# A hybrid decoder layer on one NeuronCore: SSD chunks and attention woven into the input projections, the first routing put behind chunk 0, two output projections cut into pieces

## The chip, the core and the metric

The kernel runs on one NeuronCore of one Trainium2 chip, as one launch. The metric is the device time of that launch in microseconds (us): the median of three runs.

## What is computed

One decoder layer in float32, for 512 tokens of width 1024:

```python
h = x + concat(attention, ssd) @ w_out            # of rms_norm(x) @ w_in
h = h + peer(rms_norm(h))
out = rms_norm(h)

# attention: 8 query heads, 2 key/value heads of 64, a causal window of 128, bias and sinks
# ssd: causal depthwise conv of 4 taps and silu, then a Mamba-2 scan of 8 heads in 4 chunks of 128
#      tokens: inside a chunk (CB * decay) @ X, between chunks a state; gated by silu(z), rms_norm
def peer(xn, ...):
    q = (xn @ w_query).reshape(b, s, 8, 2, 128)
    s1, s2 = q[..., 0, :] @ sub_keys1.T, q[..., 1, :] @ sub_keys2.T
    v1, i1 = top_k(s1, 16); v2, i2 = top_k(s2, 16)
    top_s, pos = top_k(v1[..., :, None] + v2[..., None, :], 16)   # of the 256 sums
    idx = i1 * 128 + i2 at pos
    # per token and head 16 experts: gelu(expert_down[idx] . xn) * softmax(top_s) * expert_up[idx]
```

For every token 8 x 16 = 128 experts are fetched. An expert is one row of 2048 floats (down and up side by side, 8 KB).

## The kernel before

The 512 tokens are four tiles of 128, one token to a partition. The work has two parts.

**Prologue.** TensorE turns x (L754) and multiplies it with w_in in blocks of 128 columns that stream through five ring buffers: 8 blocks for the convolution, a narrow one for dt (L780), 5 for keys and queries, 4 for z and 1 for v (L788, L792). Then a loop over the four chunks c (TensorE from L865, VectorE from L609, ScalarE from L350) does, in the order in which each engine's program is written, the SSD scan and the attention of the chunk, and beside them the output projection of the chunk before it (`out_half`, L811, 16 matmuls of 512 columns, L817). In chunk 2 (`ROUTED`) tile 0 is normalized, turned, and its first query is made (`query`, L829; `keyed`, L839); in chunk 3 VectorE searches the sums and writes the first indices (`search_sums`, `search_indices`). w_out (4 MB) and w_query (8 MB, one transfer into `wq`) are loaded at L224 and L225, when all projections are done.

**Expert phase.** A tile has 128 slots, the launch 512 (`NS`). For slot s GpSimd issues an indirect DMA that gathers one expert for each of the 128 tokens, 1 MB, into one of ten row buffers (L272); VectorE takes 128 dot products (`group`, L686), ScalarE their gelu (L396), VectorE the gate (L692), ScalarE a diagonal matrix (L401), and TensorE adds diagonal x up into two PSUM banks (`expert`, L955, two matmuls of 512 columns). The two matmuls release the row buffer (`row_free`). A group is 4 slots (`GROUP`). 16 slots share one query q of 32; between the groups stand the query, the keys and the search of q+2 or q+3, in pieces. Every instruction order is written out by hand; an engine runs its program in order and stops at each wait.

GpSimd has nothing but constants and the gathers, in the order of s. Before slots 0 to 6 it also waits until the buffer's earlier contents are dead; the last of these waits is for all four output projections:

```python
                elif s == 6:
                    gp.wait_ge(sem("wo_ps"), NT)
                if s >= RING_E:
                    gp.wait_ge(sem("row_free"), s - RING_E + 1)
```

## Time and profile before

| | |
|---|---|
| median of 3 runs | 1587.43 us (1584.71 to 1587.95) |
| profiled execution, its own time | 1586.41 us |
| its span in the profile | 1584.7 us |
| TensorE busy, matmul | 1378.7 us (87%) |
| VectorE / ScalarE / GpSimd busy | 1063.1 (67%) / 390.4 (25%) / 620.3 us (39%) |
| gathers | 512, 536.90 MB, 82.0% of the span of the 16 DMA engines |
| mean granted TensorE clock | 0.945 of full |

The span is the time from the first to the last instruction of the profiled execution; its own time has 1.7 us more around it. A float32 matmul shows as two records. Ends of matmuls are modelled, so a busy TensorE is not one at its peak. L numbers are lines of the kernel before.

### The profile page before, as it was taken

The page shows a single profiled execution, that of the slowest core. Times are in us where ns is not written, and L with a number is a line of the kernel's source. Part 1 is how long each engine was busy: PE and PEld are TensorE (multiplying, and loading weights), DVE is VectorE, ACT ScalarE, POOL GpSimd, SP SyncE. Part 2 cuts the span into 40 slices and gives each one's busy share as a digit, 9 for nine tenths or more (in the row PEclk, how much of TensorE's full clock was granted, in tenths as well). Part 3 has the DMA queues.
Part 4 walks back from the last instruction along what each step waited for, and adds up shares of the span by engine and source line. Part 5 has one row for each costly group of instructions (what it writes and reads, how often), then busy time and mean ns, then how long its engine had stood idle before and what let it go on. Part 6 is the DMA issues. An engine that isn't in the chain of part 4 may idle for free.

```text
span 1584.7 us, 13883 instructions
## 1 busy us (share of the span) xinstructions
PE 1378.7 (87%) x4480; PEld 721.8 (46%) x4480; DVE 1063.1 (67%) x2655; ACT 390.4 (25%) x1041; POOL 620.3 (39%) x528
## 2 busy tenths in 40 slices
PE   8899999998888888888889888888888878888787
PEld 4359776554444444444444443434444434444233
DVE  4322667687676677777767677677677777667654
ACT  2013443222222222222222221222222222222122
POOL 0000001354444454455544454444454445444541
PEclk9999999999999999899999998999999999999988
DMA  5410702999999999999999999999999999999996
GB/s 166 126 56 25 297 36 91 367 408 421 421 422 421 421 422 421 410 421 421 401 422 421 415 422 413 421 421 412 421 415 420 418 403 417 421 412 420 421 405 260
DMA packets 84380, 568.71 MB, mean 359 GB/s; under 512 B 10035, under 2 KB 12372, under 8 KB 17748
## 3 DMA queue, kind: packets, MB, share of 16 engines
q0 software_dynamic: 73728, 536.90, 82.0%
q1 hardware_dynamic: 10580, 30.93, 5.8%
q8 instruction: 35, 0.57, 0.1%
q14 instruction: 37, 0.30, 0.0%
HBM read 564.13 MB, written 3.67 MB: 358 GB/s over the span
## 4 chain that ended last, share of the span: by engine, by line
DMA 45%; PE 35%; DVE 12%; ACT 3%; issue 2%; POOL 2%; SPq 0%; DVEq 0%; ACTq 0%
DMA arena<-in_experts_du_dram,arena 42%; PE ps L955 21%; DVE arena L686 6%; PE ps L788 4%; PE ps L817 3%; POOL arena L272 2%; PE ps L792 2%; PE ps L835 2%; DMA line_scratch<-arena 2%; ACT arena L401 1%; DVE arena L692 1%; ACT arena L396 1%; ACT arena L282 1%; PE ps L937 1%; PE ps L780 1%
## 5 line engine op out<-in xcount | busy, mean ns | idle before, releaser
L955 PE MATMUL ps<-arena 128*128 128x512 f32 x2048 | 980.1, 635 | 180.3 <-ACT arena L401 179.6
L272 POOL DMA_INDIRECT arena<-in_experts_du_dram,arena x512 | 618.3, 1208 | 938.8 <-PE ps L955 604.9
L686 DVE CUSTOM_DVE_ANT_0 arena<-arena 128x1024 f32<-128x1024 f32 x512 | 618.4, 1224 | 320.2 <-DMA arena<-in_experts_du_dram,arena 314.5
L955 PEld LDWEIGHTS ps<-arena 128*128 128x128 f32 x2048 | 406.3, 203 | 711.2 <-issue 475.5
L396 ACT ACTIVATE arena<-arena 128x4 f32<-128x4 f32 (+2 forms) x131 | 26.9, 205 | 913.6 <-DVE arena L686 913.6
L401 ACT ACTIVATE arena<-ident,arena 128x128 f32<-128x128 f32 x512 | 163.9, 390 | 40.5 <-DVE arena L692 39.0
L835 PEld LDWEIGHTS ps<-arena,wq 128*128 128x128 f32 x1024 | 119.2, 192 | 15.1 <-issue 14.3
L835 PE MATMUL ps<-arena,wq 128*128 128x128 f32 x1024 | 119.6, 275 | 0.5 <-ACT arena L282 0.5
L788 PE MATMUL ps<-arena 128*128 128x512 f32 x208 | 94.7, 617 | 7.0 <-DMA arena<-in_w_in_blocks_dram 5.4
L788 PEld LDWEIGHTS ps<-arena 128*128 128x128 f32 x208 | 41.0, 199 | 59.4 <-issue 57.4
L282 ACT ACTIVATE arena<-ps 128x256 f32<-128x256 f32 (+1 forms) x114 | 51.7, 453 | 54.3 <-PE ps L835 27.9
L817 PE MATMUL ps<-arena 128*128 128x512 f32 x128 | 55.9, 594 | 1.4 <-ACT arena L282 1.4
L692 DVE SCALAR_TENSOR_TENSOR arena<-arena 128x4 f32<-128x4 f32 (+2 forms) x131 | 29.1, 222 | 38.3 <-ACT arena L396 38.3
L497 DVE TENSOR_TENSOR arena<-ps,arena 128x512 f32<-128x512 f32 x13 | 9.0, 692 | 63.7 <-PE ps L788 57.9
L686 DVE DVE_READ_ACCUMULATOR2_ANT arena<- 128x1 f32 x512 | 41.9, 82 | 0.0
L396 ACT ACT_TABLE_LOAD x32 | 41.1, 1283 | 0.6
L390 ACT ACT_TABLE_LOAD x31 | 39.8, 1283 | 0.6
L817 PEld LDWEIGHTS ps<-arena 128*128 128x128 f32 x128 | 24.0, 190 | 30.3 <-issue 28.7
L792 PE MATMUL ps<-arena 128*128 128x128 f32 x320 | 36.3, 275 | 0.0
L792 PEld LDWEIGHTS ps<-arena 128*128 128x128 f32 x320 | 36.1, 192 | 0.5 <-issue 0.5
L844 PEld LDWEIGHTS ps<-arena 128*128 128x128 f32 x128 | 19.2, 191 | 15.2 <-issue 14.8
L602 DVE TENSOR_TENSOR arena<-arena 128x512 f32<-128x512 f32 x32 | 22.5, 702 | 1.1
(153 smaller groups left out, 702.1 us busy)
## 6 DMA issues: line engine op xcount, KB each, us to landing
arena<-in_w_in_blocks_dram SPq DMA_DIRECT2D x18, 512.0 KB, 7.1
wq<-in_w_query_dram SPq DMA_DIRECT2D x1, 8192.0 KB, 33.5
arena<-in_experts_du_dram,arena POOLq DMA_INDIRECT x512
arena<-in_w_out_dram SPq DMA_DIRECT2D x1, 4096.0 KB, 14.0
h<-in_x_dram SPq DMA_DIRECT2D x4, 512.0 KB, 5.3
out_dram<-arena SPq DMA_DIRECT2D x8, 256.0 KB, 7.6
line_scratch<-arena SPq DMA_DIRECT2D x1, 1536.0 KB
arena<-line_scratch SPq DMA_DIRECT2D x1, 1024.0 KB, 5.7
```

Of the source, the lines that this page charges most:

```text
L272: gp.indirect_dma_start(rows[s % RING_E], None, experts_du, bass.IndirectOffsetOnAxis(ap=idx[:, (q // PH) % 2, q % PH * TOPK + i:q % PH * ...
L282: link(act, nc.scalar.activation(o, i, func, **kw), name, n)
L390: nc.scalar.activation(eg[:, q % 2], tdiff[:, q % 2], ACT.Exp, accum_out=gsum[:, q % 2, 0:1]).then_inc(sem("gate_exp"), 1)
L396: nc.scalar.activation(gel[:, part], pre[:, part], ACT.Gelu).then_inc(sem("gelu"), 1)
L401: nc.scalar.activation(diag[:, s % 8, :], ident[:], ACT.Copy, scale=actv[:, s % 16:s % 16 + 1]).then_inc(sem("diag"), 1)
L686: v.tensor_tensor_reduce(down, down, xn2[q // PH % 2], 1.0, 0.0, ALU.mult, ALU.add, pre[:, s % 16:s % 16 + 1]).then_inc(sem("dots"), 1)
L692: v.scalar_tensor_tensor(actv[:, part], gel[:, part], gsum[:, q % 2, 1:2], eg[:, q % 2, part], ALU.mult, ALU.mult).then_inc(sem("act_ready ...
L788: last = mm(bank[:], w[:, k, :], xnT[:, k, :], start=(k == 0), stop=(k == KT - 1))
L792: last = mm(bank[:, t * P:(t + 1) * P], xnT[:, k, t * P:(t + 1) * P], w[:, k, :], start=(k == 0), stop=(k == KT - 1))
L817: last = mm(ps[WO_BANKS[c][b]][:], mixT[c][:, k, :], wo[:, k, b * 512:(b + 1) * 512], start=(k == 0), stop=(k == KT - 1))
L835: last = mm(ps[2 + q % 2][:, j * P:(j + 1) * P], wq[:, k, col:col + P], xn2T[:, k, :], start=(k == 0), stop=(k == KT - 1))
L955: last = mm(ps[4 + 2 * (t % 2) + b][:], diag[:, s % 8, :], up[:, b * 512:(b + 1) * 512], start=False, stop=False, skip_group_check=True)
```

## The change

- **Projections.** v and dt become one step of 136 columns (`project_values`), right behind the convolution's blocks. The first block is multiplied tile by tile between the turns of x. The write of the bias line to DRAM and its reading back are two places of SyncE's order instead of one.
- **Chunks.** The loop over chunks is gone; its parts are functions that are called in a written order, and chunk 0 and the start of chunk 1 stand between the projections of k, q and z. On GpSimd four element-wise operations per chunk take work from VectorE: `skip`, `state_decay`, `add_off`, `gate`.
- **Routing.** Output projection 0 is in the middle of chunk 1; tile 0 is normalized, queried and searched during chunk 2. Slots 0 and 1 are worked off before the attention of chunk 3.
- **Output projections 2 and 3** are 32 single matmul pieces, one behind each pair of slots of the first four queries. VectorE adds a finished half to h behind the eighth pair. Output projection 1 stays whole.
- **Loads.** w_query is in eight blocks of 1 MB. 0 and 1 are loaded in the projections, 2 and 3 before the first gather, 4 and 5 when slots 1 and 2 are free, 6 and 7 and the two norm weights of 512 KB behind the last output projection.
- **Buffers.** Twelve row buffers: slots 0 to 9 use ten of them once, slots 10 to 65 go round eight (`EARLY_RING`), slots from 66 (`JOIN`) round ten (`FULL_RING`). Buffers 10 and 11 lie where w_out was; slot 66 waits for the last output projection.
- **Groups** have 2 slots in the first four queries, then 4 as before. In the expert phase query and keys are made for q+2 (before: q+3), and the first two thirds of the search stand in one piece behind the last group.

```diff
+HALF_RING = 8
+JOIN = 66
+N_BUF = 12
+def buffer_of(s):
+    if s < 10:
+        return s
+    if s < JOIN:
+        return EARLY_RING[(s - 10) % HALF_RING]
+    return FULL_RING[(s - JOIN) % 10]
+EARLY_RING = [0, 3, 4, 5, 6, 7, 8, 9]
+FULL_RING = [10, 11, 0, 3, 4, 5, 6, 7, 8, 9]
+    _sizes = [2] * 8 if _q < 4 else [4] * 4 if _q < NQ - 1 else [4, 4, 2, 2, 2, 1, 1]
...
 SyncE
+            for q in (4, 5):
+                sp.wait_ge(sem("row_free"), q - 2)
+                sp.dma_start(w_head[q], w_query[q].rearrange("p (k c) -> p k c", k=KT)).then_inc(sem(f"wq_in{q}"), 16)
+            sp.wait_ge(sem("wo_half"), 2 * NT)
+            for q in (6, 7):
+                sp.dma_start(w_head[q], w_query[q].rearrange("p (k c) -> p k c", k=KT)).then_inc(sem(f"wq_in{q}"), 16)
+            sp.dma_start(w_ffn, norm_ffn.to_broadcast([P, D])).then_inc(sem("wffn_in"), 16)
             sp.dma_start(w_fin, norm_final.to_broadcast([P, D])).then_inc(sem("wffn_in"), 16)
...
 GpSimd
+            def gate(c):
+                gp.wait_ge(sem("diag_read"), c + 1)
+                gp.wait_ge(sem("zv_out"), NT * NT)
+                link(gp, g.tensor_tensor(yb[:, c, :], yb[:, c, :], zs[c], ALU.mult), "gated", n)
...
-                elif s == 6:
-                    gp.wait_ge(sem("wo_ps"), NT)
-                if s >= RING_E:
-                    gp.wait_ge(sem("row_free"), s - RING_E + 1)
+                elif s == 3:
+                    gp.wait_ge(sem("mixS_ready"), NT)
...
+                elif s == 6:
+                    gp.wait_ge(sem("pv_ps"), NT)
+                elif s == 8:
+                    gp.wait_ge(sem("mixS_ps"), NT)
+                elif s == JOIN:
+                    gp.wait_ge(sem("wo_half"), 2 * NT)
+                if LAST_USER[s] is not None:
+                    gp.wait_ge(sem("row_free"), LAST_USER[s] + 1)
...
 VectorE, the expert phase
+            def add_projection(c, b):
+                dve.wait_ge(sem("wo_half"), 2 * c + b + 1)
+                half = slice(512 * b, 512 * b + 512)
+                go(v.tensor_tensor(h[:, c, half], h[:, c, half], ps[WO_BANKS[c][b]][:], ALU.add), "h_mixed")
...
             for q in range(NQ):
                 t, r = divmod(q, PH)
+                for i, (s0, n_slots) in enumerate(GROUPS[q]):
+                    if s0:
+                        group(q, s0, n_slots)
+                    done = s0 + n_slots - q * TOPK
+                    if t == 0 and r < 4 and i % 8 == 7:
+                        add_projection(2 + r // 2, r % 2)
+                    if done == 4 and q and q + 1 < NQ:
+                        search_indices(q + 1)
...
+                    if done == 16:
+                        if q + 2 < NQ:
+                            search_halves(q + 2)
+                            search_sums(q + 2)
...
 TensorE, the end of the prologue and the expert phase
+            turn_mix(2)
+            ssd_diagonal(3)
+            out_half(1, 0)
+            add_residual(0)
+            experts(*GROUPS[0][0])
+            turn_probs(3)
+            attend(3)
+            out_half(1, 1)
+            turn_mix(3)
             for q in range(NQ):
                 t, r = divmod(q, PH)
+                for i, (s0, n_slots) in enumerate(GROUPS[q]):
+                    if s0:
+                        experts(s0, n_slots)
+                    if t == 0 and r < 4:
+                        out_piece(2 + r // 2, r % 2, i)
+                    done = s0 + n_slots - q * TOPK
+                    if done == 4 and q + 2 < NQ:
+                        query(q + 2)
+                    if done == 8 and q + 2 < NQ:
+                        keyed(q + 2)
```

**GpSimd, from the constants to the gathers.** Rows give a line, an operation, tiles written and read, size and the semaphores waited for. Before:

```order
L251 MEMSET arena 128x3 [waits const] x8
L272 DMA arena<-in_experts_du_dram,arena 128x2048 [waits nat_ps,routed,const]
L272 DMA arena<-in_experts_du_dram,arena 128x2048 [waits score_sb]
L272 DMA arena<-in_experts_du_dram,arena 128x2048 [waits y_ps]
L272 DMA arena<-in_experts_du_dram,arena 128x2048 [waits pv_ps]
L272 DMA arena<-in_experts_du_dram,arena 128x2048 [waits mixT_ps]
L272 DMA arena<-in_experts_du_dram,arena 128x2048
L272 DMA arena<-in_experts_du_dram,arena 128x2048 [waits wo_ps]
```

Now, from `skip(3)` to the gather of slot 8 (`wide` and `arena` hold the row buffers):

```order
L317 TENSOR_TENSOR wide<-arena,hrow 128x512 [waits nat_sb,gated]
L359 DMA wide<-in_experts_du_dram,arena 128x2048 [waits step_ps,routed,y_skip]
L359 DMA arena<-in_experts_du_dram,arena 128x2048 x2
L324 TENSOR_TENSOR state<-state,sm 128x512 [waits state_ready,decays,off_ps]
L330 TENSOR_TENSOR wide<-wide,arena 128x512 [waits off_read,state_dec]
L336 TENSOR_TENSOR wide<-wide,arena 128x512 [waits zv_out,diag_read,y_off]
L359 DMA wide<-in_experts_du_dram,arena 128x2048 [waits mixS_ready,gated]
L359 DMA arena<-in_experts_du_dram,arena 128x2048 [waits score_sb]
L359 DMA arena<-in_experts_du_dram,arena 128x2048 [waits y_ps]
L359 DMA arena<-in_experts_du_dram,arena 128x2048 [waits pv_ps]
L359 DMA arena<-in_experts_du_dram,arena 128x2048
L359 DMA arena<-in_experts_du_dram,arena 128x2048 [waits mixS_ps]
```

Three gathers stand ahead of the last chunk's operations, the others behind them, and the chunk's norm (`mixS_ready`) is waited for by slot 3.

**VectorE, between the last slots of a query and the first of the next, in the first four queries.** Each `ISA arena<-arena 128x1024` is the dot product of one slot. Before (the last group of query 0, the halves of a search, the next group):

```order
L686 ISA arena<-arena 128x1024 [waits row5]
L686 ISA arena 128x1
L692 SCALAR_TENSOR_TENSOR arena<-arena 128x4 [waits gelu]
L569 MAX arena<-arena 128x8 [waits s_sb]
...
L584 CAST arena<-arena 128x32 [waits half1,half0]
L686 ISA arena<-arena 128x1024 [waits row6,dve_step]
```

Now (the last pair of query 1, the finished half, the search, the next pair):

```order
L852 SCALAR_TENSOR_TENSOR arena<-arena 128x2 [waits gelu]
L775 TENSOR_TENSOR h<-h,ps 128x512 [waits wo_half]
L800 MAX arena<-arena 128x8 [waits s_sb,h_mixed]
...
L818 TENSOR_TENSOR arena<-arena 128x256 [waits dve_step]
...
L826 TENSOR_SCALAR arena<-arena 128x16 [waits dve_step]
L846 ISA arena<-arena 128x1024 [waits row8]
L846 ISA arena 128x1
L846 ISA arena<-arena 128x1024 [waits row9]
L846 ISA arena 128x1
L850 RECIPROCAL arena<-arena 128x1 [waits gate_exp]
L852 SCALAR_TENSOR_TENSOR arena<-arena 128x2 [waits gelu,dve_step]
```

The add that waits for `wo_half` stands ahead of the search and of the next query's first pair.

**TensorE at the same place** (L1193 the experts, four rows to a pair; L1142 a piece of an output projection). Before there is no output projection in this stretch (L955 the experts). Now:

```order
L1193 MATMUL ps<-arena 128x512 x4
L1142 MATMUL ps<-wide,arena 128x512
L1193 MATMUL ps<-wide,arena 128x512 x4
L1142 MATMUL ps<-wide,arena 128x512
L1193 MATMUL ps<-arena 128x512 x4
L1142 MATMUL ps<-wide,arena 128x512
L1171 MATMUL ps<-arena 128x128 x16
```

The eighth piece of a half, which raises `wo_half`, comes behind the eighth pair of its query, and the next pair follows at once.

## Rows read from the trace of the kernel before

**Rows 1.** The page: GB/s in 40 slices of 39.6 us, and the chain's shares.

```profile
GB/s 166 126 56 25 297 36 91 367 408 421 421 422 421 421 422 421 410 421 421 401 422 421 415 422 413 421 421 412 421 415 420 418 403 417 421 412 420 421 405 260
...
DMA 45%; PE 35%; DVE 12%; ACT 3%; issue 2%; POOL 2%; SPq 0%; DVEq 0%; ACTq 0%
```

**Rows 2.** Busy time by window: engines' us and counts, clock granted, DMA share, GB/s.

```profile
0.00:294.00 294.00, 275.51 (x1317) 183.08 (x1318) 143.55 (x341) 81.01 (x190) 12.33 (x26) 0.98 0.37 124
...
314.00:318.00 4.00, 4.00 (x6) 1.87 (x7) 3.93 (x7) 1.07 (x4) 0.24 (x1) 0.62 1.02 426
```

**Rows 3.** Timeline of GpSimd: start, us, what, idle before and releaser.

```profile
1.09 0.29 POOL L245 TENSOR_SCALAR_AFFINE_SELECT ident<-ones 128x128 f32<-128x128 f32 x1
...
265.82 1.53 POOL L272 DMA_INDIRECT arena<-in_experts_du_dram,arena  x1 [262.60 <-DVE arena L606]
...
288.68 0.94 POOL L272 DMA_INDIRECT arena<-in_experts_du_dram,arena  x1 [13.02 <-PE ps L817]
...
1559.45 0.94 POOL L272 DMA_INDIRECT arena<-in_experts_du_dram,arena  x1 [0.78 <-PE ps L955]
```

**Rows 4.** Timeline of VectorE: dot products of slots 6, 66, 510 and 511.

```profile
294.19 1.22 DVE L686 CUSTOM_DVE_ANT_0 arena<-arena 128x1024 f32<-128x1024 f32 x1 [4.25 <-DMA arena<-in_experts_du_dram,arena]
...
447.28 1.23 DVE L686 CUSTOM_DVE_ANT_0 arena<-arena 128x1024 f32<-128x1024 f32 x1 [1.25 <-DMA arena<-in_experts_du_dram,arena]
...
1570.62 1.23 DVE L686 CUSTOM_DVE_ANT_0 arena<-arena 128x1024 f32<-128x1024 f32 x1 [0.72 <-DMA arena<-in_experts_du_dram,arena]
...
1573.08 1.22 DVE L686 CUSTOM_DVE_ANT_0 arena<-arena 128x1024 f32<-128x1024 f32 x1 [0.74 <-DMA arena<-in_experts_du_dram,arena]
```

**Rows 5.** Timeline of TensorE (two records to a matmul).

```profile
4.41 1.94 PE L754 MATMUL ps<-ident,h 128*128 128x128 f32 x8 [4.41 <-DMA h<-in_x_dram]
7.50 5.38 PE L754 MATMUL ps<-ident,h 128*128 128x128 f32 x24 [1.15 <-DMA h<-in_x_dram]
...
79.30 8.49 PE L780 MATMUL ps<-arena 128*128 128x8 f32 x64
...
251.75 13.95 PE L817 MATMUL ps<-arena 128*128 128x512 f32 x32
...
288.24 3.73 PE L835 MATMUL ps<-arena,wq 128*128 128x128 f32 x32
...
293.53 0.61 PE L844 MATMUL ps<-arena 128*128 128x128 f32 x4
293.98 13.90 PE L955 MATMUL ps<-arena 128*128 128x512 f32 x32
...
443.77 15.48 PE L955 MATMUL ps<-arena 128*128 128x512 f32 x32 [4.54 <-ACT arena L401]
```

**Rows 6.** Timeline of VectorE: chunk work (segments, norm from first to last, scores, maxima).

```profile
192.33 0.69 DVE L668 CUSTOM_DVE_ANT_0 arena<-arena 128x512 f32<-128x512 f32 x1
...
195.16 0.75 DVE L670 SCALAR_TENSOR_TENSOR arena<-arena,sm,wn 128x512 f32<-128x512 f32 x1
...
208.73 2.15 DVE L627 TENSOR_SCALAR arena<-ps,sm 128x128 f32<-128x128 f32 x8
...
215.33 2.87 DVE L650 SCALAR_TENSOR_TENSOR arena<-ps,arena 128x512 f32<-128x512 f32 x4
218.23 2.29 DVE L652 TENSOR_REDUCE sm<-arena 128x8 f32<-128x2048 f32 x1
```

**Rows 7.** Timeline of VectorE: a search from first to last, an add, a dot's end.

```profile
299.32 0.48 DVE L569 MAX8 arena<-arena 128x8 f32<-128x128 f32 x2
...
305.22 0.43 DVE L595 TENSOR_SCALAR arena<-arena 128x16 f32<-128x16 f32 x1
...
308.12 0.17 DVE L606 SCALAR_TENSOR_TENSOR arena<-arena 128x16 int32<-128x16 f32 x1
...
313.41 0.68 DVE L547 TENSOR_TENSOR h<-h,ps 128x512 f32<-128x512 f32 x1
...
441.50 1.22 DVE L686 CUSTOM_DVE_ANT_0 arena<-arena 128x1024 f32<-128x1024 f32 x1
```

More of the change, by code:

```diff
@@ L39 @@
 SLOTS = PH * TOPK
-GROUP = 4
-RING_E = 10
 NS = 4 * SLOTS
@@ new lines, in _ @@
+            values()
+            dt_exps()
+            ssd_start(0)
+            ssd_decay(0)
+            softmax(0)
+            gates_z(0)
+            gates_z(1)
+            turned(0)
+            ssd_start(1)
+            gates_z(2)
+            gates_z(3)
+            ssd_decay(1)
+            mixed(0)
+            softmax(1)
+            squared(0)
+            turned(1)
+            ssd_start(2)
+            transposed(0)
+            ssd_decay(2)
+            query(0)
+            softmax(2)
@@ new lines, in scores @@
+            def scores(c, part):
+                k0 = 0 if c else P
+                if c and part == 0:
+                    dve.wait_ge(sem("pv_ps"), c)
+                if c == 0 and part == 0:
+                    dve.wait_ge(sem("bias_in"), 16)
+                dve.wait_ge(sem("score_ps"), 2 * c + part + 1)
+                for i in range(2):
+                    b = 2 * part + i
+                    src = ps[B_ATT[i]][:].rearrange("p (h k) -> p h k", h=2)
+                    go(v.scalar_tensor_tensor(prob[:, 2 * b:2 * b + 2, k0:], src[:, :, k0:], float(HD) ** -0.5,
+                                              bias[:, 2 * b:2 * b + 2, k0:], ALU.mult, ALU.add), "score_sb")
@@ L749, in _, with turn_x @@
             pe.wait_ge(sem("const"), LOADS["const"])
-            for t in range(NT):
+            def turn_x(t):
                 pe.wait_ge(sem(f"x_in{t}"), 16)
@@ new lines, in _ @@
+            mm(ps[4][0:HEADS, 0:LW], rb[:], buckets, start=True, stop=True).then_inc(sem("line_ps"), 1)
+            for n_step in range(1, NXB):
+                project(n_step)
+            project_values()
+            project(S_K)
+            ssd_start(0)
+            project(S_Q)
+            ssd_segments(0)
+            ssd_state(0)
+            project(S_Q + 1)
+            ssd_diagonal(0)
+            project(S_Q + 2)
+            project(S_Q + 3)
+            scores(0, 0)
+            scores(0, 1)
@@ new lines, in _ @@
+            project(S_Z)
+            project(S_Z + 1)
+            turn_probs(0)
+            attend(0)
+            project(S_Z + 2)
+            ssd_start(1)
+            scores(1, 0)
+            project(S_Z + 3)
+            ssd_segments(1)
+            scores(1, 1)
+            turn_mix(0)
+            ssd_off(1)
+            ssd_state(1)
+            out_half(0, 0)
+            ssd_diagonal(1)
+            out_half(0, 1)
+            turn_probs(1)
+            attend(1)
+            ssd_start(2)
@@ new lines, in _ @@
+            transpose_normed(0)
+            scores(2, 0)
+            query(0)
+            ssd_segments(2)
+            scores(2, 1)
+            keyed(0)
+            ssd_off(2)
+            ssd_state(2)
+            turn_mix(1)
+            query(1)
+            ssd_diagonal(2)
+            keyed(1)
+            turn_probs(2)
+            attend(2)
+            ssd_start(3)
+            scores(3, 0)
+            ssd_segments(3)
+            scores(3, 1)
+            ssd_off(3)
+            ssd_state(3)
@@ L974, in _ @@
[L974 to L995 removed]
+                if t and r == 0:
+                    add_residual(t)
```

1103 lines of the change are left out of this document (607 added, 496 removed).

## The prediction

> **What bounds the kernel now.** I read the page first [rows 1]. In its slices DMA moves little for 260 us but for one load of weights, then some 420 GB/s to the end, and the chain that ended last lies 45% in DMA. So there are two stretches. In the first, TensorE is the bound: of the first 294 us it is busy 275.5 [rows 2]. In the second, the gathers are. At the end the dot products of slots 510 and 511 start 2.46 us apart [rows 4], 1 MB of 128 x 8 KB rows each. Between slot 66 (447.3) and slot 511 (1573.1) a slot takes 1125.8 / 445 = 2.53 us; the excess over 2.46 is stores and the like.
>
> From this follows how the change is to be read. Once the stream of gathers runs without a gap, the end is fixed by how many slots have landed at what time and how many other bytes go through the same engines. Work that TensorE does beside it is free as long as it doesn't hold up `row_free`. The first gather starts at 265.8, slot 6 is issued at 288.7 [rows 3], and slot 66 has landed at 447.3 [rows 4].
>
> Slot 66 is also where the change has its gate: its gather waits for all eight halves of the output projections, and GpSimd is in order, so nothing behind it goes out either. Before that only slots up to 65 can have been fetched. **The forecast is therefore the time E at which TensorE finishes the last piece**, compared with 447.3.
>
> **When TensorE enters the expert loop.** Its work up to there is that of before up to 294, 275.5 us [rows 2], less the dt step (8.5), less output projections 2 and 3 (2 x 13.95), plus two slots (16 matmuls, 8 slots, take 13.9, so 1.74 each) [rows 5]: 275.5 - 8.5 - 27.9 + 3.5 = 242.6. The wider v step adds about 0.5: 243.
>
> To this come waits, which I get by walking the written orders of TensorE and VectorE side by side. The waits for x stay: 4.4 + 1.2 = 5.6 [rows 5]. Four larger ones are new, since chunk work that used to be hidden behind 14 us of output projection now has little beside it:
> - Chunk 1, behind the last z block: four Silu copies, GpSimd's `gate(0)`, VectorE's norm (192.3 to 195.9, 3.6) and the first segments (half of 2.15) [rows 6], then the copies of the turned mix. Against it stand some 4 us of TensorE work. Wait 5.1.
> - Before the first `keyed`: VectorE has half the scores (1.4), the maxima with their three small steps (2.9), the segments (2.15) [rows 6], then ScalarE an exponential and the copy of the query, which stands behind it in its order. TensorE has nothing. Wait 7.8.
> - Chunk 3, before `ssd_off(3)`: norm of chunk 2, scores, maxima and first segments, less what TensorE has beside it. Wait 7.5.
> - Before the first expert: search of query 1 (299.3 to 308.3, 9.0) [rows 7], norm 3.6, a pair of dots 2.4 and 1.0 to the first matmul, 16 in all, against 8.9 of output projection 1 and residual. Wait 8.2.
>
> The sum is 28.6. Eight small ones (the reciprocal norms of x behind the tile-wise first block, the dt chain of 9 us behind a k block of 7, turns of the probabilities, the norm of tile 0) I estimate from rows of the same kind at 15.0 together. One more cost: after a wait of 4.5 us, eight slots took 15.5 instead of 13.9, 1.6 more [rows 5], and a stretch that follows such a wait has a granted clock of 0.62 [rows 2], between the two levels of 1.2 and 2.4 GHz. Three of the waits are long enough: 5. Entry: 243 + 5.6 + 43.6 + 5 = 297, where before the first expert starts at 294.0.
>
> The earlier routing shows little of itself here. By the same walk the first gather starts near 241, 24 us earlier, but it is followed by only two more. Slot 3 lies in the buffer that holds y, so it waits for the last norm, which VectorE does behind the search of query 1: about 270. Slot 6 waits for the last attention (285 to 290), slot 8 for the turned mix (near 297).
>
> GpSimd's element-wise operations of 128 x 512 don't occur before. From below VectorE's similar one is 0.69 (L668) [rows 6]; from above, four of GpSimd's own 128-column selects are 1.16 [rows 3]. I take 1.2, the engine's own row; only `gate(0)` and two others lie on the path, so either end moves E by 1 us. The Trainium skill (GPSIMD Engine Reference, section Performance versus the Vector engine) gives 2.6 cycles an element for two inputs; by it an estimate is 1.1 us, and the sum would be the same.
>
> **From the entry to E.** Query 0: 14 slots 24.4, eight pieces at 0.87 (16 take 14.0) 7.0, a query 3.7, its keys 0.6 [rows 5], and 1.8 for the first pair's dots: 37.5, so 335. Query 1 to 3 each 16 x 1.74 + 7.0 + 3.7 + 0.6 = 39.1 of TensorE work. That is as much as 16 gathers (39.4), so TensorE would be just fast enough.
>
> But between the queries there is a **ring of waits**. VectorE adds the finished half behind its eighth pair, and that add waits for the eighth piece, which TensorE does behind its own eighth pair. VectorE, some 10 us ahead by then, stands still until TensorE has caught up. Only then come the add (0.7), the two parts of the search that stand in one piece (299.3 to 305.65, less a little, 6.2) and the first pair's dots (2.4), and 1.0 later (dots from 441.5, 1.22 long, matmul at 443.8) TensorE's next matmul [rows 5, 7]. TensorE has nothing else in its order: it idles 10.4 us, and then runs slow for 1.7. Before, the searches are cut in three between groups and no add depends on TensorE's last work. A query takes 39.1 + 10.4 + 1.7 = 51.2, three take 153.6. **E = 335 + 153.6 = 488.6.**
>
> In that time DMA runs dry again and again: eight buffers are full within 20 us and none is released in the gap. Blocks 4 and 5 of w_query go there for nothing.
>
> **From E to the end.** At E at most slots up to 65 have landed. Slot 66 is issued and lands 5.5 us later, as slot 6 did out of an idle stream (288.7 to 294.2) [rows 3, 4]: 494.1, against 447.3: +46.8. With it go w_query 6 and 7 and the norm weights, 3 MB; before, the same bytes were moved ahead of slot 6, where DMA had a hole. At 2.46 a MB: +7.4. From there the stream has eight gathers and 3 MB queued (27 us), enough to cover the next gap, and everything behind it is as before: groups of 4, ten buffers, the same tail. The longer undivided search delays a release by 3 us; a gather goes out some 13 us before its dots start (the last 1559.5 and 1573.1) [rows 3, 4], five rows deep, which covers it: 0.
>
> The change is +54.2. On the profiled execution's own 1586.4 us that is 1640.6; the median of the runs shown is 1.0 above it: **1641 us**.
>
> A page speaks against this step: the Trainium skill (DMA: Bandwidth & Descriptors, section Specifications) sets 358 GB/s as a core's HBM limit. The slices show 421 for most of the phase [rows 1], above it, so the measured rate stands; by 358 the 3 MB would take 8.8 instead of 7.4, and the sum would be 1642.
>
> **Rivals.**
> - *The gaps are hidden.* VectorE's hold costs nothing because the next pair is ready before TensorE gets there. Then a query takes 39.1 to 40, E = 335 + 119 = 454, and the result 1641 - 35 = 1606. For it: before, VectorE does keep ahead. Against it: the written order has the add first, with its wait. 0.12.
> - *Faster than before.* The start 24 us earlier is carried to the end, as it would be if slots 3 to 65 streamed without a gap and the pieces kept pace. Less the 7.4 of loads: 1587.4 - 24 + 7.4 = 1571. It decides at E: the break-even is 447.3 - 5.5 - 7.4 = 434, 55 before my E. Against it: TensorE alone needs 297 + 37.5 + 117 from the waits as I have them; even with none of the 43.6 it is 408 and DMA must have no gap either. 0.05.
> - *GpSimd pays for switching.* It alternates between element-wise work and gathers. The Trainium skill (GPSIMD Engine Reference, section Architecture, Instruction dispatch) has about 6 us for the first call of newly loaded code. As a mechanism here: `state_decay(3)` stands between gathers and VectorE waits for it, so a stall would go into the entry. The nearest row is the first gather, 1.53 against 0.94 for a later one [rows 3], so nothing of that size is seen so far; with 6 us, 1647. 0.05.
>
> My forecast has 0.78. The range: its own terms give 1625 to 1657 (the walk's 43.6 us of waits by a third either way, the gap of 10.4 by a few tenths, three times). It is reached down to 1604 to take in the hidden gaps, which leaves out the fast case and tails. Below 0.2%, 3 us, a measurement of this kernel can't be told from no change. Faster 0.05; the same 0.02, for a walk that is wrong by just the whole sum; slower 0.93.
>
> **What would show it.** Right: TensorE idle three or four times for about 10 us, released by ScalarE's diagonal, some 50 us apart, between 330 and 490; VectorE's add waiting about as long for TensorE each time; DMA slices between 240 and 490 well under full; the gather of slot 66 issued near 489. The first gather near 241 and the fourth near 270 show the walk right. Wrong: DMA full from 300 on, or slot 66 fetched before 450.

## The result and the profile after

The changed kernel takes **1664.1 us** (median of 4, 1662.0 to 1666.5) against 1587.7 for the kernel before on the same chip: a ratio of **1.048 (1.046 to 1.050)**. The profiled execution has 1663.43 us and a span of 1661.7, where before had 1584.7: +77.0. The forecast was 1641 with a range of 1604 to 1657. The kernel is slower, as forecast, but it lies above the range, by 23 us from the forecast; one term of the prediction's sum was too small (see below).

The page of the changed kernel, in its 40 slices (now 41.5 us each), and the shares of the chain that ended last, against [rows 1]:

```profile
PEclk9998978889987899999999999999989999999999
...
GB/s 166 164 164 13 38 26 76 254 337 376 304 310 343 415 410 421 419 423 421 421 415 395 418 421 421 422 417 416 422 389 422 421 422 422 416 412 422 421 421 274
...
PE 48%; DVE 24%; DMA 20%; issue 3%; ACT 3%; POOL 2%; SPq 0%; DVEq 0%; ACTq 0%; POOLq 0%
```

The gathers' stream is full (421 GB/s) only from some 540 us on; before it was so from 320. DMA's share of the chain fell from 45% to 20%. TensorE's timeline shows where the time went (start, duration, line, and in brackets the idle time ahead and its releaser):

```profile
26.24 1.12 PE L1224 MATMUL ps<-arena,ones 128*128 128x512 f32 x2 [2.73 <-ACT arena L388]
...
28.57 51.14 PE L985 MATMUL ps<-arena 128*128 128x512 f32 x112
...
184.72 1.12 PE L1126 MATMUL ps<-ident,arena 128*128 128x128 f32 x4 [3.42 <-DVE arena L738]
...
218.32 1.77 PE L1154 MATMUL ps<-ident,arena 128*128 128x128 f32 x8 [3.70 <-DVE arena L786]
...
241.52 1.22 PE L1184 MATMUL ps<-arena 128*128 128x128 f32 x4 [7.84 <-ACT arena L388]
...
274.27 2.08 PE L1046 MATMUL ps<-state,arena 128*128 128x256 f32 x4 [7.17 <-DVE arena L698]
...
298.30 3.78 PE L1193 MATMUL ps<-wide,arena 128*128 128x512 f32 x4 [7.99 <-ACT arena L524]
...
319.91 1.10 PE L1142 MATMUL ps<-wide,arena 128*128 128x512 f32 x2 [1.03 <-ACT arena L388]
...
366.64 6.43 PE L1193 MATMUL ps<-arena 128*128 128x512 f32 x8 [10.06 <-ACT arena L524]
...
418.05 6.33 PE L1193 MATMUL ps<-arena 128*128 128x512 f32 x8 [10.06 <-ACT arena L524]
...
469.35 6.28 PE L1193 MATMUL ps<-arena 128*128 128x512 f32 x8 [10.05 <-ACT arena L524]
...
509.53 1.02 PE L1142 MATMUL ps<-wide,arena 128*128 128x512 f32 x2
526.68 6.63 PE L1193 MATMUL ps<-arena 128*128 128x512 f32 x8 [16.13 <-ACT arena L524]
```

(The row at 28.57 is steps 1 to 7.) The row at 319.91 is the first piece of output projection 2, the entry of the loop. Behind it come three gaps of 10.06 us, 51.4 us apart, and a fourth of 16 behind the last piece (the row at 509.53, done at 510.6; this is the prediction's E). In VectorE's timeline the ring of waits stands in the forecast order: the add waits 7.24 us for TensorE's eighth piece (L1142), the search stands behind it, then the dots, then one short wait for ScalarE:

```profile
356.62 0.69 DVE L775 TENSOR_TENSOR h<-h,ps 128x512 f32<-128x512 f32 x1 [7.24 <-PE ps L1142]
...
363.22 1.22 DVE L846 CUSTOM_DVE_ANT_0 arena<-arena 128x1024 f32<-128x1024 f32 x1
...
365.94 0.22 DVE L852 SCALAR_TENSOR_TENSOR arena<-arena 128x2 f32<-128x2 f32 x1 [0.27 <-ACT arena L515]
...
520.40 1.23 DVE L846 CUSTOM_DVE_ANT_0 wide<-wide,arena 128x1024 f32<-128x1024 f32 x1 [0.63 <-DMA wide<-in_experts_du_dram,arena]
```

The last row is slot 66, which had landed at 447.3 before [rows 4]: 73.1 us later. GpSimd's timeline, against [rows 3]: the first gather, the fourth, the seventh (slot 6) and slot 66.

```profile
256.87 1.26 POOL L336 TENSOR_TENSOR wide<-wide,arena 128x512 f32<-128x512 f32 x1 [9.88 <-issue]
261.52 1.54 POOL L317 TENSOR_TENSOR wide<-arena,hrow 128x512 f32<-128x512 f32 x1 [3.39 <-ACT arena L388]
263.34 1.27 POOL L359 DMA_INDIRECT wide<-in_experts_du_dram,arena  x1 [0.29 <-POOL wide L317]
...
295.60 1.34 POOL L359 DMA_INDIRECT wide<-in_experts_du_dram,arena  x1 [11.75 <-DVE arena L738]
...
311.36 0.94 POOL L359 DMA_INDIRECT arena<-in_experts_du_dram,arena  x1 [11.93 <-PE ps L1111]
...
510.82 0.94 POOL L359 DMA_INDIRECT wide<-in_experts_du_dram,arena  x1 [11.98 <-PE ps L1142]
```

**The whole loss as bytes.** Both kernels move 568.7 MB and run at 421 GB/s in most slices later on (417 as the mean from 600 to 1500 us, in both). So the loss should be the bytes that are not yet moved when both are there. The windows of each kernel (GB/s is the last number), before, then after:

```profile
0.00:560.00 560.00, 509.72 (x2044) 302.48 (x2044) 345.54 (x868) 147.50 (x369) 142.08 (x133) 0.96 0.67 264
```

```profile
0.00:560.00 560.00, 455.94 (x1786) 277.17 (x1787) 277.26 (x699) 134.06 (x336) 119.06 (x116) 0.90 0.55 206
```

(264 - 206) x 0.56 = 32.5 MB, at 421 GB/s 77.1 us; the spans differ by 77.0. Nothing behind 560 us has to take part. For the eleven kernels below that move the same bytes (all but e6) the same sum agrees with the spans to 2 us. It says how large a loss is and by when it has arisen, not what made it.

### The profile page after: what moved, and what is told of

The parts are those of the page before. It is cut to its first block, busy times and chain, and to the rows that moved or that the text cites. A ratio compares the mean times of both kernels' runs of the same rounds, so it can differ in the third digit from the quotient of the medians.

```text
span 1661.7 us, 13951 instructions
## 1 busy us (share of the span) xinstructions
PE 1384.7 (83%) x4464; PEld 730.6 (44%) x4464; DVE 1055.3 (64%) x2659; ACT 398.7 (24%) x1059; POOL 640.4 (39%) x542
## 4 chain that ended last, share of the span: by engine, by line
PE 48%; DVE 24%; DMA 20%; issue 3%; ACT 3%; POOL 2%; SPq 0%; DVEq 0%; ACTq 0%; POOLq 0%
PE ps L1193 27%; DMA arena<-in_experts_du_dram,arena 11%; DMA wide<-in_experts_du_dram,arena 9%; PE ps L1171 7%; DVE arena L846 6%; PE ps L985 5%; DVE wide L846 4%; PE ps L1142 3%; PE ps L989 2%; DVE arena L812 1%; ACT arena L388 1%; DVE arena L806 1%; DVE arena L803 1%; DVE arena L825 1%; DVE arena L822 1%
## 5 line engine op out<-in xcount | busy, mean ns | idle before, releaser
L1193 PE MATMUL ps<-arena 128*128 128x512 f32 x1264 | 610.1, 634 | 142.4 <-ACT arena L524 142.4
L359 POOL DMA_INDIRECT arena<-in_experts_du_dram,arena x316 | 379.7, 1202 | 460.0 <-PE ps L1193 422.0
L846 DVE CUSTOM_DVE_ANT_0 arena<-arena 128x1024 f32<-128x1024 f32 x316 | 380.5, 1224 | 192.2 <-DMA arena<-in_experts_du_dram,arena 191.3
L1193 PEld LDWEIGHTS ps<-arena 128*128 128x128 f32 x1264 | 250.7, 204 | 467.0 <-issue 290.4
L1193 PE MATMUL ps<-wide,arena 128*128 128x512 f32 x784 | 377.5, 632 | 83.3 <-ACT arena L524 83.1
L359 POOL DMA_INDIRECT wide<-in_experts_du_dram,arena x196 | 241.4, 1232 | 278.6 <-PE ps L1193 240.6
L846 DVE CUSTOM_DVE_ANT_0 wide<-wide,arena 128x1024 f32<-128x1024 f32 x196 | 236.3, 1224 | 117.4 <-DMA wide<-in_experts_du_dram,arena 116.9
L1193 PEld LDWEIGHTS ps<-wide,arena 128*128 128x128 f32 x784 | 154.9, 203 | 284.7 <-issue 180.8
L985 PE MATMUL ps<-arena 128*128 128x512 f32 x192 | 86.2, 609 | 0.0
L388 ACT ACTIVATE arena<-ps 128x256 f32<-128x256 f32 (+1 forms) x114 | 52.2, 458 | 134.0 <-PE ps L1171 84.6
L1171 PEld LDWEIGHTS ps<-arena,wide 128*128 128x128 f32 x512 | 61.9, 198 | 7.3 <-issue 7.3
L1171 PEld LDWEIGHTS ps<-arena 128*128 128x128 f32 x512 | 59.7, 192 | 7.7 <-issue 7.7
L1142 PE MATMUL ps<-wide,arena 128*128 128x512 f32 x128 | 61.1, 595 | 2.0 <-ACT arena L388 2.0
L1171 PE MATMUL ps<-arena,wide 128*128 128x128 f32 x512 | 62.3, 282 | 0.0
L985 PEld LDWEIGHTS ps<-arena 128*128 128x128 f32 x192 | 37.3, 196 | 46.5 <-issue 46.0
## 6 DMA issues: line engine op xcount, KB each, us to landing
out_dram<-arena SPq DMA_DIRECT2D x8, 256.0 KB, 7.8
```

The source lines that it names most:

```text
L359: gp.indirect_dma_start(rows[b], None, experts_du, bass.IndirectOffsetOnAxis(ap=idx[:, (q // PH) % 2, q % PH * TOPK + i:q % PH * TOPK + i ...
L388: link(act, nc.scalar.activation(o, i, func, **kw), name, n)
L846: v.tensor_tensor_reduce(down, down, xn2[q // PH % 2], 1.0, 0.0, ALU.mult, ALU.add, pre[:, s % 16:s % 16 + 1]).then_inc(sem("dots"), 1)
L985: last = mm(bank[:], w[:, k, :], xnT[:, k, :], start=(k == 0), stop=(k == KT - 1))
L1142: ins = mm(ps[WO_BANKS[c][b]][:], mixT[c][:, k, :], wo[:, k, b * 512:(b + 1) * 512], start=(k == 0), stop=(k == KT - 1), skip_group_check= ...
L1171: last = mm(ps[query_bank(q)][:, j * P:(j + 1) * P], w[:, k, j * P:(j + 1) * P], xn2T[:, k, :], start=(k == 0), stop=(k == KT - 1))
```

## The experiments

The kernel before ran beside each of them, at medians of 1586.8 to 1588.6. Times are medians; "less" is against the changed kernel's 1664.1 where nothing else is said. The entry of the loop also moves by itself: in the five kernels whose program is the same up to there (the changed one, e1, e2, e3 gaps, e4) it is at 317.3 to 322.5 us, each in one profile. So the shifts of the entry below are good to some 3 us.

**e1: the add behind the search.** Theory: the ring of waits makes the gaps. Rival: gathers through eight buffers set the pace.

```diff
-                    if t == 0 and r < 4 and i % 8 == 7:
-                        add_projection(2 + r // 2, r % 2)
...
                             search_sums(q + 2)
+                        if t == 0 and r < 4:
+                            add_projection(2 + r // 2, r % 2)
```

> The changed kernel, but VectorE's add of the finished half stands behind both parts of the next search instead of ahead of them. Ring of waits: the search (6.2 us) is then done while TensorE still works, and the gap holds only the add (0.7), the pair's dots (2.4) and 1.0: TensorE's three gaps of 10.06 us shrink to about 4, the restart costs less than 2.8, E moves from 510 to about 491, and the time goes down by 18 to 22 us, to about 1644. Rival (the period of 51.4 us is set by the gathers through eight buffers, and the gap only shows it): the gaps are filled by waits on rows, the period and the time stay within 3 us.

Measured 1645.58 (ratio 1.036, 1.033 to 1.039): 18.5 less. TensorE's rows at the first two gaps:

```profile
363.37 5.40 PE L1193 MATMUL ps<-arena 128*128 128x512 f32 x8 [4.19 <-ACT arena L524]
...
407.87 5.40 PE L1193 MATMUL ps<-arena 128*128 128x512 f32 x8 [4.18 <-ACT arena L524]
```

The gap is 4.19 and the period 44.5: just the search (5.9) and 1.0 of the slow restart have left it. The period follows the gap, so the rival, that the gathers set it, falls.

**e2: the add in the next query.**

```diff
-                    if t == 0 and r < 4 and i % 8 == 7:
-                        add_projection(2 + r // 2, r % 2)
+                    if t == 0 and 0 < r < 5 and done == (6 if r < 4 else 4):
+                        add_projection(2 + (r - 1) // 2, (r - 1) % 2)
```

> The changed kernel, but the add of each finished half is put off until after the third pair of the next query, so VectorE depends on no work of TensorE that is still to come. Ring of waits: no gap of 10 us is left, nor a slow restart; a query takes TensorE's own 39 to 40 us instead of 51.4, the entry stays at 320, E is at about 475, and the time is 30 to 36 us lower, about 1631. Rival (gathers through eight buffers set the pace): the period stays above 45 us and the time is less than 15 us lower.

Measured 1631.49 (1.029, 1.025 to 1.032): 32.6 less. Of the gaps one of 2.21 us stays, and the last piece is done at 477.4. The window of 460 to 480 us now shows a hole in DMA (share 0.64) in a stream that is full on both sides (1.01 from 340 to 460 and from 480 to 520), and behind the last piece TensorE idles 17 us:

```profile
358.44 3.70 PE L1193 MATMUL ps<-arena 128*128 128x512 f32 x8 [2.21 <-ACT arena L524]
...
494.35 5.47 PE L1193 MATMUL ps<-arena 128*128 128x512 f32 x8 [16.98 <-ACT arena L524]
```

```profile
460.00:480.00 20.00, 17.36 (x42) 7.45 (x41) 13.18 (x41) 2.67 (x9) 4.39 (x5) 1.00 0.64 259
```

**e4: the join at slot 74.** The hole should be the gate: slot 66 waits for the last piece.

```diff
-JOIN = 66
+JOIN = 74
```

> The kernel with the adds put off (e2_add_in_next_query), and the two buffers that the output weights occupy taken into the ring at slot 74 instead of 66, so slot 66 no longer waits for the last piece of the projections. In e2 the DMA share is 1.01 from 340 to 460 us, 0.64 from 460 to 480, and 1.00 after. If that hole is the gate's, it closes: 20 x 0.36 = 7 us less than e2's 1631.5, so about 1624, and TensorE's idle time of 17 us behind the last piece goes. Rival (eight buffers can't keep the queue full while TensorE works through the pieces, so the hole stays or moves on): within 2 us of e2.

Measured 1625.58 (1.024, 1.021 to 1.026): 5.9 less than e2 by the medians, 7.6 by the spans (1629.3 and 1621.7). The hole is closed, and TensorE's idle time of 17 us is 3.6:

```profile
460.00:480.00 20.00, 17.54 (x44) 7.62 (x42) 14.44 (x46) 2.17 (x7) 11.32 (x9) 1.00 1.01 411
```

The 17 us of idle TensorE were worth only 7: in this phase the bytes count, not TensorE.

**e3, gaps: unused matmuls in the gaps.** Here the question is the clock.

```diff
+            def fill(bank, n):
+                for _ in range(n):
+                    mm(ps[bank][:], ident[:], wn[:], start=True, stop=True)
...
+                if q < 3:
+                    pe.wait_ge(sem("s_sb"), q + 2)
+                    fill((q + 1) % 2, 10)
```

> The changed kernel with ten more matmuls of 512 columns, whose result nothing reads, in each of the three gaps of 10 us between queries 0 to 3. Clock theory: the first pair behind a gap takes 3.6 us again instead of 6.4, so E is some 8 us earlier, about 502, and the time 6 to 9 us lower. Rival (the first pair is slow because its rows or its diagonal are late, not because of the clock): the time stays within 2 us, or is up to 2 us longer where the extra matmuls outlast the gap.

Measured 1655.18 (1.043, 1.040 to 1.046): 8.9 less. The fill, and the first pair behind it:

```profile
353.83 8.75 PE L1216 MATMUL ps<-wn,ident 128*128 128x512 f32 x20
364.04 3.70 PE L1193 MATMUL ps<-arena 128*128 128x512 f32 x8 [1.47 <-ACT arena L524]
```

3.70 where the changed kernel has 6.43 behind a gap of 10.06. The pair starts 10.05 us behind the eighth piece's end, where it is 10.06 in the changed kernel, so its rows and diagonal came no earlier; it was the clock. Three times 2.7 is 8.1.

**e3, prologue: unused matmuls in the three largest waits** (`fill(1, 7)` before `keyed(0)`, before `ssd_off(3)`, here behind a wait for ScalarE's copy of a query's scores, and before the first experts).

> The changed kernel with seven more matmuls of 512 columns (0.87 us each at the full clock), whose result nothing reads, in each of TensorE's three largest waits ahead of the expert loop: before keyed(0), before ssd_off(3), before the first expert. If the 22 us by which the prediction fell short are mostly TensorE working at half the clock behind its waits, the granted clock from 220 to 320 rises above 0.90 and the first pass of the expert loop starts 5 to 12 us earlier, and the time is as much lower. Rival (the waits themselves are longer than I had them, the clock is a side effect): the entry stays within 2 us or gets later by up to 4, as the extra matmuls delay what they stand before.

Measured 1655.97 (1.043, 1.041 to 1.046): 8.1 less, the entry at 313.4, 6.5 earlier. The windows of the changed kernel and then of this one:

```profile
240.00:280.00 40.00, 30.37 (x185) 26.67 (x186) 29.41 (x82) 17.56 (x50) 10.77 (x9) 0.80 0.22 80
280.00:320.00 40.00, 30.61 (x116) 17.07 (x116) 18.27 (x62) 8.48 (x19) 7.20 (x7) 0.87 0.42 158
```

```profile
240.00:280.00 40.00, 36.25 (x220) 28.12 (x219) 32.80 (x94) 19.60 (x55) 11.94 (x10) 1.00 0.21 80
280.00:320.00 40.00, 35.25 (x122) 18.16 (x121) 22.24 (x64) 8.85 (x20) 9.45 (x10) 1.00 0.53 201
```

The granted clock goes from 0.80 and 0.87 to 1.00 (2.4 GHz). Not all was mended: from 200 to 240 us it is 0.74, and 0.82 in the changed kernel.

**e5: real work in the waits.** Output projection 1's halves each one place earlier.

```diff
             scores(3, 1)
+            out_half(1, 0)
             ssd_off(3)
...
             ssd_diagonal(3)
-            out_half(1, 0)
+            out_half(1, 1)
             add_residual(0)
...
             attend(3)
-            out_half(1, 1)
```

> The changed kernel with the two halves of output projection 1 one place earlier each in TensorE's order: half (1,0) ahead of ssd_off(3), into its wait of 7.2 us, and half (1,1) ahead of the first experts instead of behind attend(3). If the waits hold TensorE up because nothing is left to put there, and VectorE sets their end, the first expert still starts near 298 and the entry of the loop is 7 to 9 us earlier (about 312), and so is the end: about 1656. Rival (TensorE's work ahead is on VectorE's path, so the wait before the first expert grows by what the other loses): the entry and the time stay within 2 us.

Measured 1653.59 (1.042, 1.039 to 1.044): 10.5 less. The first expert and the entry, 3.7 and 10.3 us earlier than in the changed kernel:

```profile
294.64 3.78 PE L1193 MATMUL ps<-wide,arena 128*128 128x512 f32 x4 [8.11 <-ACT arena L524]
...
309.59 1.10 PE L1142 MATMUL ps<-wide,arena 128*128 128x512 f32 x2 [1.03 <-ACT arena L388]
```

The wait before the first expert has not grown; the one before `ssd_off(3)` has no row any more, and that step (2.08 above, behind 7.17 of idle time) runs at the full clock:

```profile
272.82 1.13 PE L1046 MATMUL ps<-state,arena 128*128 128x256 f32 x4
```

The 3.7 at the first expert were not expected. Some 1.5 of them are there ahead of the edit already (the second scores of chunk 3 start at 263.66 and at 265.11); the rest fits the faster work of chunk 3.

**e6: without the loads of w_query 6 and 7.** Queries 6 and 7 of each tile multiply by what lies in that place.

```diff
-            for q in (6, 7):
-                sp.dma_start(w_head[q], w_query[q].rearrange("p (k c) -> p k c", k=KT)).then_inc(sem(f"wq_in{q}"), 16)
```

> The changed kernel without the loads of blocks 6 and 7 of w_query (2 MB), which the change has behind the last piece; queries 6, 7 and their like multiply by what lies in that place. By the prediction these bytes go through a full stream, at 2.46 us a MB: 4.9 us less, about 1659. Rival (they fall into idle DMA time behind the gate and cost nothing): within 2 us of 1664.

Measured 1659.26 (1.044, 1.042 to 1.047): 4.8 less, as 2 MB in a full stream would cost. The traces give less. From the gather of slot 66 to the end the seven kernels with JOIN = 66 and all 3 MB (the changed one, e1, e2, both e3, e5, e8) take 1150.6 to 1151.7 us, though that gather goes out anywhere from 477.6 to 510.8. Here it goes out at 509.02, 1.8 earlier than in the changed kernel, and 1148.1 are left:

```profile
509.02 0.94 POOL L357 DMA_INDIRECT wide<-in_experts_du_dram,arena  x1 [12.29 <-PE ps L1140]
```

By these traces the 2 MB cost 2.5 to 3.6 us, less than 2.46 a MB. They are not free, so the rival falls; the price itself stays between 1.3 and 2.4 us a MB.

**e8: the first block in one piece.**

```diff
-            turn_x(0)
-            turn_x(1)
-            pe.wait_ge(sem("ring0"), 16)
-            project_tile(0)
...
+            for t in range(NT):
+                turn_x(t)
+            pe.wait_ge(sem("xT_sb"), 2 * NT)
+            project(0)
```

> The changed kernel with its first projection block in one piece of 512 columns behind all four transposes of x, as before, instead of tile by tile. In the trace step 1 starts at 28.57 us where my walk had 24.6 (before 23.1). If these 4 us are the tile-wise block's (sixteen 128-column matmuls a tile at half the clock), step 1 starts at 23 to 25, the entry of the loop and the end come 4 to 5.5 us earlier, about 1659.5. Rival (VectorE's convolution, not TensorE, sets the pace of the first eight blocks): within 2 us of 1664.

Measured 1657.28 (1.044, 1.042 to 1.046): 6.8 less, more than I gave it. Steps 1 to 7, against 28.57 and 51.14 above, and the entry (319.91 above):

```profile
23.35 48.50 PE L985 MATMUL ps<-arena 128*128 128x512 f32 x112
...
312.33 1.10 PE L1142 MATMUL ps<-wide,arena 128*128 128x512 f32 x2 [1.03 <-ACT arena L388]
```

Step 1 comes 5.2 us earlier, and the same 112 records take 2.6 less, since in the changed kernel they begin behind a wait of 2.73 us, on a slow clock (granted from 28 to 80 us: 0.94, here 1.00). This part of the change costs 7.6 us of entry by itself.

**e9: all together** (e4's kernel, e5's and e8's edits, 3 unused matmuls ahead of `transpose_normed(0)`, 7 ahead of `keyed(0)`).

> The changed kernel with everything so far: adds put off, join at slot 74, halves of projection 1 moved into the waits, whole first block, and unused matmuls in the waits ahead of transpose_normed(0) (3) and keyed(0) (7). If the losses are additive terms of one path (entry, gaps, gate), the sum is 1664 - 32.6 - 5.9 - 10.5 - 4.5 - 3 = about 1607, and the kernel is still 15 to 20 us slower than before, because the entry (about 300) leaves eight pieces of output projection for a time in which TensorE has just the gathers' pace. Rival (the stream of gathers was already full in e4, so an earlier entry only moves waits): 1616 or more.

Measured 1610.53 (1.014, 1.012 to 1.015), 3.5 above the sum as it was expected. With e8's measured 6.8 in place of 4.5 the sum is 1605, so 5 us of the terms overlap. The kernel is still 23 slower than before. The entry is at 300.7. Its window:

```profile
0.00:560.00 560.00, 494.09 (x1883) 288.31 (x1884) 319.52 (x812) 145.86 (x369) 141.22 (x136) 0.95 0.63 244
```

(264 - 244) x 0.56 = 11.2 MB, 26.6 us (the spans differ by 24.8). Of this, 7.8 MB were missing at 300 us already (104 GB/s against 130 over 0 to 300), the others behind it (405 against 419 over 300 to 560). Some 4 MB of them are w_query 5 to 7 and two norm weights, which before were loaded by then (issued from 168.7 to 271.0 us) and here are issued at some 305 and at 466, into a stream that now has no holes: 10 us. The rest is gathers, of which only eight have been issued by 300 us (before: 13). That split was worked out, not tried.

**e7 and e10: two parts of the change in the kernel before.** e7 takes the order of the bias lines (written behind block 6, waited for behind block 9); e10 takes the merged v and dt step as well.

```diff
-                if b == 5:
+                if b == 6:
                     sp.wait_ge(sem("line_done"), 1)
...
+                if b == 9:
                     sp.wait_ge(sem("line_out"), 16)
```

```diff
-B_K, B_Q, B_Z, B_V = NXB, NXB + 1, NXB + 5, NXB + 9
+B_K, B_Q, B_Z = NXB, NXB + 1, NXB + 5
...
-                            last = mm(bank[:, t * SH:(t + 1) * SH], xnT[:, k, t * P:(t + 1) * P], w_dt_sb[:, k, :],
+                            last = mm(ps[6 + t // 2][:, t % 2 * VW:(t % 2 + 1) * VW], xnT[:, k, t * P:(t + 1) * P],
+                                      w_vd_sb[:, k, :],
```

> The kernel before, with one thing of the change alone: SyncE writes the bias lines behind block 6 and waits for them only behind block 9, instead of both behind block 5. TensorE's wait of 5.4 us for its sixth block (63.1 us) goes. TensorE is the bound until the gathers start, so the time is 5 to 8 us lower than before's 1588, about 1582. Rival (the later steps wait for VectorE's convolution anyway, so the wait moves to there): within 2 us of before.

> The kernel before with two parts of the change alone: the order of the bias lines (as e7) and the merged step for v and dt (136 columns; 8.5 us of dt step and 7 us of v step become 7.6). TensorE does 8 us less ahead of the first gather, but the v step no longer stands behind chunk 0's diagonal as cover. If the TensorE time is what counts there: 6 to 8 us less than e7, about 1576 to 1577. Rival (the cover was needed: softmax of chunk 0 and its turns now show as a wait): within 2 us of e7's 1583.

e7: 1583.48 against 1588.63, ratio 0.997 (0.996 to 0.999); TensorE's wait of 5.41 us at 63.1 is gone. e10: 1573.08 against 1587.57, **0.991 (0.989 to 0.993)**. The merged step gives 9 to 10 us, more than the 8 of TensorE's work it saves; without the v step as cover a wait of 2.2 us came for 1.35:

```profile
153.31 2.00 PE L937 MATMUL ps<-arena 128*128 128x64 f32 x16 [2.20 <-ACT arena L284]
```

What the last 1 to 2 us are I did not find. By bytes e10 is (276 - 264) x 0.56 = 6.7 MB or 16 us ahead; the spans say 15.0.

**e11: output weights freed in pairs** (e10's kernel; projection 3 runs over k outside and halves inside, and gathers 6 to 9 wait for one pair of row blocks each).

```diff
-            for b in range(2):
-                out_half(NT - 1, b)
+            for k in range(KT):
+                for b in range(2):
+                    last = mm(...)
+                if k % 2:
+                    last.then_inc(sem("wo_ps" if k == KT - 1 else "wo_pair"), 1)
```

> The kernel of e10, with output projection 3 taken row block by row block for both halves, so that the buffers of gathers 6 to 9, which lie in the output weights, come free one by one from 3.5 us after the start of its 14 us, instead of all at its end. In e10 gather 6 is issued at 273.8 and the DMA share from 260 to 280 us is 0.78. If that hole counts, gather 6 is issued near 263 and the time falls by up to 20 x 0.22 = 4.4 us, to about 1569 to 1571. Rival (slot 10 waits for the first expert, at 281, whatever slots 6 to 9 do, so the hole only moves to 270 to 281): within 1.5 us of 1573.

Measured 1570.27 against 1586.76: **0.989 (0.987 to 0.991)**, whose interval overlaps that of e10, so the gain of some 2 us over e10 stays unclear. Slot 6 and slot 10 in e10 and then in e11:

```profile
273.79 0.94 POOL L274 DMA_INDIRECT arena<-in_experts_du_dram,arena  x1 [12.64 <-PE ps L820]
...
281.25 0.94 POOL L274 DMA_INDIRECT arena<-in_experts_du_dram,arena  x1 [2.78 <-PE ps L955]
```

```profile
265.96 0.94 POOL L276 DMA_INDIRECT arena<-in_experts_du_dram,arena  x1 [2.54 <-PE ps L966]
...
283.72 0.94 POOL L276 DMA_INDIRECT arena<-in_experts_du_dram,arena  x1 [6.52 <-PE ps L957]
```

Slot 6 goes 7.8 us earlier, but slot 10 waits for the first expert in both and goes 2.5 us later: the hole moved partly to there, as the rival had it. e10 and e11 beat both kernels.

## Why the prediction was right and wrong

- **What bounds it, and where to look.** Right: the loss is the stream of gathers that starts full later, and nothing behind 560 us. That the time of the last piece fixes the end is borne out by the seven kernels named at e6: whatever moved that piece, 1151 us were left behind it. *Faster than before* falls with it: slot 66 was fetched 73 us later, not 24 earlier.
- **Ring of waits.** Right in place, order and size: gaps of 10.06 (10.4 forecast), 51.4 us apart (51.2). The slow restart was 2.8 and not 1.7; a query's own work, 38.5 and not 39.1, and the shorter gap make up for it. VectorE's add waited 7.24 us, not about 10. From the entry to E it took 190.6 us, where the steps gave 191. e1 shortens the ring and gets 18.5 back, e2 takes it away and gets 32.6; that the gaps were hidden falls.
- **The four larger waits.** 7.84, 7.17 and 7.99 against 7.8, 7.5 and 8.2; the wait of 5.1 is 3.42 and, a little later, 0.97. Right.
- **Entry: the step that failed.** 297 forecast, 319.9 measured. These 22.9 us are all of the error of E (488.6 forecast, 510.6 measured) and of the end. The row says which half of the sum it was:

```profile
0.00:320.00 320.00, 267.84 (x1245) 184.67 (x1246) 140.43 (x356) 81.08 (x191) 28.38 (x39) 0.90 0.31 104
```

  The waits are 320 - 267.8 = 52.2; I had 49.2. The busy time is 267.8; I had 243 and 5 for the clock, 20 less. At a mean granted clock of 0.90 it is by estimate some 241 at the full one: the work was counted rightly to a few us, and the term of the clock ("Three of the waits are long enough: 5") was mis-sized; it measured some 25 (267.8 - 243). Waits that I held to be too short cost clock as well (steps 1 to 7: 2.6 behind a wait of 2.73). The trace of before had shown it: the stretch at a clock of 0.62 that I cited [rows 2] doesn't follow the wait of 4.5 us but this one of 2.54, behind which 16 records take 8.65 us instead of 7.03, the same 1.6:

```profile
313.98 8.65 PE L955 MATMUL ps<-arena 128*128 128x512 f32 x16 [2.54 <-ACT arena L401]
```

  The changed prologue has four waits of 2.7 to 3.7 us beside the three large ones. At 1.6 to 2.8 us each these seven come to 11 to 20 by estimate. The runs bear it out in part: filling three waits with unused matmuls made the entry 6.5 earlier, and of the shifts only this one is clock alone. e8 gave 7.6, e5 10.3, all together 19.3, each less certain by the 3 us or so that the entry moves by itself. How much of e5's and e8's is clock and how much wait stays open, so some 7 of the 20 us are shown by a run and the rest by the busy time at its granted clock.
- **First block tile by tile.** The walk had step 1 at 24.6, it is 28.57; I had priced it with the waits for x at nothing of its own.
- **Routing earlier.** The first gather was forecast at 241 and goes out at 263.3, 2.5 us earlier than before; the fourth was forecast at 270 and goes out at 295.6. Both were my own signs that the walk was right, and both say that it was not. The first one's indices are ready at 256.0 (VectorE's L837 at 255.84): by there the walk is 15 us late. The other 7 are GpSimd's order: `gate(2)` and `skip(3)` stand ahead of it, and `skip(3)` waits for ScalarE's copy in chunk 3 [the rows at 256.87 and 261.52]. That was there to be read in the order and I did not count it. By the walk's own reasoning it cost little, since only three gathers stand there; no run tried it.
- **From E to the end.** Slot 66's dots start 9.6 us behind its issue and not 5.5, with 3 MB of loads issued beside it (8.9 in e6, with 1 MB); what was left of the loads' cost then came to 3.9 and not 7.4 (77.0 - 73.1). The two together were forecast at 12.9 and are 13.5. By e6's trace 2 of the 3 MB account for 2.5 to 3.6 us where the forecast had 4.9, so the sum is right partly by luck, and a part of it has another cause, which stays open.
- **GpSimd.** 1.2 us for its 128 x 512 operations: 1.04 to 1.55 measured, mostly 1.27. Right. The two gathers right behind such work take 1.27 and 1.34 us, the ones behind them 0.94; before, without such operations, gathers take 0.93 to 1.99, the first 1.53. The first gather starts 0.29 us behind `skip(3)`. So there is no switching cost, and that rival falls. The 6 us that the Trainium skill has for the first call of newly loaded code (GPSIMD Engine Reference, section Architecture, Instruction dispatch) show here neither in a row nor as idle time ahead of one.
- **The range.** It allowed a third of the 43.6 us of waits either way, and nothing for the clock on 243 us of work. That was the uncertain number. Two sums are rounded a little off: the ring's steps give 10.3, not 10.4, and 1640.6 + 1.0 is 1641.6.

## What to carry to other kernels

When a stream of transfers sets the end, sum the bytes that are missing at the time from which both kernels run full; that gives the difference before any mechanism is named, and shows which part of the program can matter. In a written order, never let an engine that runs ahead wait for the last piece of the one that follows it before it has issued what the follower needs next; put the add one turn later. When a change cuts cover away, price the busy time of the part at the clock that a stretch with such waits shows, not only the waits; and try each part of a large change alone, since here two small parts were worth 14.5 us in the kernel before, while the whole change costs 76.

## What the runs showed of the hardware

- TensorE's first pair behind idle time (3.60 us at the full clock): 3.70 behind 2.21 idle, 5.40 behind 4.19, 6.43 behind 10.06, and 3.70 again when the 10 us were filled with matmuls that nobody reads. The length of the wait alone does not set the price: 3.70 behind 3.57 (e4), 5.47 behind 16.98 (e2), and in the kernel before 1.6 us lost behind 2.54. Useless work in a wait made the kernel 8 to 9 us faster, twice.
- In stretches of 40 us with such waits, between 200 and 320 us, the mean granted clock was 0.72 (e1) to 0.87, between the two levels of 1.2 and 2.4 GHz, and a prologue with some 241 us of work at the full clock (an estimate, 267.8 x 0.90) took 267.8 busy.
- The full stream of row gathers moves 421 GB/s in most slices of every one of these kernels. The Trainium skill gives some 358 as a core's HBM limit, as half of a stack's 716 (DMA: Bandwidth & Descriptors, section Specifications); this kernel, alone on one core, moves more, and what two cores at once would get no run here shows.
- From the issue of slot 66's gather to its dots it took 9.6 to 10.6 us with 3 MB of plain loads beside it (seven kernels), 8.9 with 1 MB (e6), and 5.5 out of an idle stream (slot 6 before).
